# The recurrence's token shift split between ScalarE and VectorE, with a new order table

## The reference, cut to what matters

```
shifted = concatenate([prev[:, None], p[:, :-1]])      # the token before
xs = p + (shifted - p) * mu                            # mu: one weight per projection column
```

## Time and profile before

| what | us |
|---|---|
| median of 3 runs | 2172.32 (2167.52 to 2173.0) |
| the profiled execution's own time | 2170.53 |
| its span, first to last instruction | 2168.6 |
| interleaved stage, layer 1 | 412.8 |
| interleaved stage, layer 2 | 410.8 |

### The profile page before, as it was taken

How to read it: one execution, slowest core, us unless ns; L and a number is a source line. 1 busy time by engine, 2 the same in 40 slices (tenths; PEclk the granted TensorE clock), 3 DMA queues, 4 the chain that set the end, 5 groups by cost and what they waited for, 6 DMA issues and landing times.

```text
span 2168.6 us, 53451 instructions
## 1 busy us (share of the span) xinstructions
PE 1960.5 (90%) x22324; PEld 1804.1 (83%) x22324; DVE 1231.5 (57%) x2034; ACT 702.4 (32%) x1294; POOL 49.2 (2%) x137
## 2 busy tenths in 40 slices
PE   5999999988896999999769998999887979999995
PEld 5999888766696999999769987887666879999995
DVE  3254888887736444452333448888886364444423
ACT  3222333433334232342233223433334332222421
POOL 0000000000000101100000000000000000110000
PEclk9999899998998999999879998999998979999998
DMA  4224733232321323223132256332333212323232
GB/s 181 89 84 144 180 109 105 61 99 83 106 94 45 93 89 97 88 88 98 53 133 89 78 176 160 99 99 71 101 88 110 82 49 89 98 88 96 81 101 79
DMA packets 155835, 214.36 MB, mean 99 GB/s; under 512 B 21569, under 2 KB 121410, under 8 KB 153922
## 3 DMA queue, kind: packets, MB, share of 16 engines
q1 hardware_dynamic: 151682, 208.64, 31.5%
q10 hardware_dynamic: 3904, 2.23, 0.5%
HBM read 202.57 MB, written 16.59 MB: 101 GB/s over the span
## 4 chain that ended last, share of the span: by engine, by line
PE 64%; DVE 18%; SPq 8%; issue 4%; ACT 3%; DMA 3%; DVEq 0%; ACTq 0%; another core or an unknown queue 0%
PE ps L814 17%; PE ps L816 16%; PE ps L815 16%; SPq L704 7%; PE ps L1166 2%; DMA ring<-in_w 1%; DVE arena L1999 1%; PE ps L833 1%; DVE arena L1767 1%; DVE arena L1990 1%; PE ps L834 1%; DVE x L2179 1%; DVE arena L1904 1%; PE ps L1132 1%; PE ps L1047 1%
## 5 line engine op out<-in xcount | busy, mean ns | idle before, releaser
L1678 DVE TENSOR_TENSOR ring_lo<-ring,ring_hi 128x1024 fp32r<-128x1024 f32 x202 | 247.4, 1225 | 679.9 <-ACT ring_hi L1321 679.4
L814 PE MATMUL ps<-hm_hi,ring_hi 128*128 128x260 f32 x1600 | 456.1, 285 | 10.0 <-DVE hm_lo L1685 5.2
L816 PE MATMUL ps<-hm_hi,ring_lo 128*128 128x260 f32 x1600 | 454.7, 284 | 0.0
L815 PE MATMUL ps<-hm_lo,ring_hi 128*128 128x260 f32 x1600 | 453.3, 283 | 0.0
L1321 ACT ACTIVATE ring_hi<-ring 128x1024 fp32r<-128x1024 f32 x202 | 213.8, 1059 | 680.2 <-PE ps L816 615.7
L814 PEld LDWEIGHTS ps<-hm_hi,ring_hi 128*128 128x128 f32 x1600 | 304.1, 190 | 12.5 <-issue 7.3
L816 PEld LDWEIGHTS ps<-hm_hi,ring_lo 128*128 128x128 f32 x1600 | 303.7, 190 | 0.0
L815 PEld LDWEIGHTS ps<-hm_lo,ring_hi 128*128 128x128 f32 x1600 | 303.7, 190 | 0.0
L814 PE MATMUL ps<-in_hi,ring_hi 128*128 128x260 f32 x736 | 211.6, 287 | 6.9 <-DVE ring_lo L1678 6.9
L814 PE MATMUL ps<-hf_hi,ring_hi 128*128 128x260 f32 x704 | 202.1, 287 | 8.8 <-DVE hf_lo L1685 8.2
L816 PE MATMUL ps<-in_hi,ring_lo 128*128 128x260 f32 x736 | 207.8, 282 | 0.0
(11 more groups left out here) (401 smaller groups left out, 3354.5 us busy)
## 6 DMA issues: line engine op xcount, KB each, us to landing
ring<-in_w SPq DMA_DIRECT2D x202, 512.0 KB, 3.5
extra<-in_kv_cmp SPq DMA_DIRECT2D x96, 128.0 KB, 2.3
arena<-in_kv_cmp SPq DMA_DIRECT2D x80, 128.0 KB, 2.4
slot<-in_kv_cmp SPq DMA_DIRECT2D x80, 128.0 KB, 2.9
out_win_old<-in_win SPq DMA_DIRECT2D x16, 511.0 KB, 4.4
arena<-in_k_sel SPq DMA_DIRECT2D x96, 64.0 KB, 1.9
extra<-in_k_sel SPq DMA_DIRECT2D x96, 64.0 KB, 1.9
slot<-in_v_sel SPq DMA_DIRECT2D x96, 64.0 KB, 1.9
```

Source lines behind the costliest of these rows:

```text
L814: mmul(out, wh, hi[:, k, cols], start=(k == 0), stop=False)
L815: mmul(out, wh, lo[:, k, cols], start=False, stop=False)
L816: last = mmul(out, wl, hi[:, k, cols], start=False, stop=(ci == len(chunks) - 1 and k == k1 - 1))
L1678: v.tensor_tensor(ring_lo[:, n % RING, :], r, ring_hi[:, n % RING_HI, :], SUB).then_inc(S["w_lo"], 1)
```

## The change

The token shift becomes `xs = p * (1 - mu) + shifted * mu`. `dif` leaves VectorE. A new ScalarE step `part` computes the first product into the tile `dif`, 14 copies of 128 columns, each scaled by a per-partition operand; `mix` and `mixlow` become 2 and 12 scalar_tensor_tensor of 128 columns, shifted times mu plus `dif`. `mix` waits for `part` on a new semaphore `part1`; `part` of slice sc waits for the key squares of slice sc - 1 (for slice 0: for `rs out`). `1 - mu` is made once per layer by one VectorE instruction into a new tile `rest_mu`; the arena shrinks by 20 columns. The planner's costs: `dif` 4.25 (VectorE) becomes `part` 4.2 (ScalarE), `mix` 0.85 becomes 0.6, `mixlow` 1.9 becomes 2.6.

```
-        put("dif", "DVE", 4.25)
+        put("part", "ACT", 4.2, *([ago("squares")] if sc else []))
-        put("mix", "DVE", 0.85, *([ago("rkv")] if sc else []))
+        put("mix", "DVE", 0.6, *([ago("rkv")] if sc else []), *here("part"))
-        put("mixlow", "DVE", 1.9, *here("mix"))
+        put("mixlow", "DVE", 2.6, *here("mix"))
...
-ORDER = ("008670667870768677066086067707700667767767777666070707668676070667786607700000777701716817177181767106167171718776717171"
+ORDER = ("067680866070870767607678076007676770676767767060867770667768670067676660077006066760870767661671176186610171766767867117"
...
+        rest_mu = sb("rest_mu", [P, RP])
...
-        ARENA = 30900
+        ARENA = 30880
...
-                    if stage == "tanh":
+                    if stage == "part":
+                        if sc:
+                            act.wait_ge(T["x1"], 2 * sc)
+                        else:
+                            act.wait_ge(S["rs_out"], 1)
+                        for i in range(RP):
+                            o.go(A(dif[:, i, :], pr[:, i, sc * SC + 1:(sc + 1) * SC + 1], ACT.Copy, scale=rest_mu[:, i:i + 1]))
+                        o.tell(T["part1"])
+                    elif stage == "tanh":
...
+                o.go(v.tensor_scalar(rest_mu[:], C("mu"), -1.0, 1.0, MUL, ADD))
...
-                    if stage == "dif":
-                        o.do(v.tensor_tensor(dif, pr[:, :, sc * SC:(sc + 1) * SC], pr[:, :, sc * SC + 1:(sc + 1) * SC + 1], SUB))
-                        o.go(v.tensor_tensor(dif, dif, wide(C("mu"), SC), MUL))
...
+                    if stage in ("mix", "mixlow"):
+                        if stage == "mix":
+                            dve.wait_ge(*at_sc("part1", 1))
+                        for i in range(3 * RJ, RP) if stage == "mix" else range(3 * RJ):
+                            o.go(v.scalar_tensor_tensor(xs[:, i, :], pr[:, i, sc * SC:(sc + 1) * SC], C("mu", i), dif[:, i, :], MUL, ADD))
+                        if stage == "mix":
+                            o.tell(T["x1"])
+                        else:
+                            o.settle()
```

More of the change, by code:

```diff
@@ L138, in constants @@
     return c, np.concatenate([cos, sin], 1)
-PER_SC = {"x1": 2, "act1": 2, "lora1": 2, "sig1": 2, "ld_ok": 1, "kk1": 2, "gl_mm": 1, "y_mm": 2, "gg_ok": 1, "rk_ok": 2, "root1": 1, "exp1": 1, "prep": 2,
+PER_SC = {"x1": 2, "part1": 1, "act1": 2, "lora1": 2, "sig1": 2, "ld_ok": 1, "kk1": 2, "gl_mm": 1, "y_mm": 2, "gg_ok": 1, "rk_ok": 2, "root1": 1, "exp1": 1, "prep": 2,
           "gmm": 4, "gmask": 4, "nmm": 1, "inv_q": LEVELS - 1, "inv_qc": LEVELS - 1,
@@ L353, in early_thread @@
     return [(("early", 0, "whi"), "ACT", 1.15, [("smp", 6, "sel_v")]), (("early", 0, "wlo"), "DVE", 1.4, [("early", 0, "whi")])]
-ORDER = ("008670667870768677066086067707700667767767777666070707668676070667786607700000777701716817177181767106167171718776717171"
[L357 to L362, removed]
+ORDER = ("067680866070870767607678076007676770676767767060867770667768670067676660077006066760870767661671176186610171766767867117"
+         "617767617617167776161776276373322672326227233662237672322366722367272662762638216667262712762627118621621617622176826176"
+         "122612166272727762776726278271122721276272672273427277146427672747272786436743232687343767232367762377266683772773716167"
+         "166277767861626671676227776622776662172761276167672627617616827627277616276767268277278676218727226672671622771222687622"
+         "627672466362427241277462764262223682243273328622363782662246662662327832637223611221862116122612712861126218721282622211"
+         "262227277626627626727427272242678727726722276622747767227462662662238276482267363263326722364262726232322487263266272226"
+         "323622262464866744686677645647547776")
 def merged_order():
```

## The result

Over 20 runs each, the changed kernel takes 2175.0 us (2168.7 to 2181.3) and the kernel before 2170.6: ratio 1.0017, 95% interval 1.0009 to 1.0025. It is slower by a little, inside what I called no change and inside the range; the forecast had been faster, 2162.5.

The account below looks back on a forecast made before the run. PE was taken to bound the stage up to win_v 0, SP's load issue most of the rest. Per layer +5.1 - 9.1 = -4.0 us, -8.0 for two, from 2170.5 to 2162.5 us; range 2147 to 2178.

Parts of the forecast that it names:

- The frame: Interleaved stage, once per layer: its end was put 168.2 us behind win_v 0, plus SP's stall ahead of unit 31.
- C: Selected-key softmax, 497.4 to 537.5 us: less VectorE work ahead of sel_v 0 ends SP's stall, -9.1 us a layer (0 to -10.6).
- A: Stage up to win_v 0, at 421.5 us: PE bounds it and gets 8.8 us more, 3.7 taken back: +5.1 a layer.
- VectorE loses 7.2 there and gains 11.5: Ahead of win_v 0: three slices save VectorE 2.4 us each, moved steps add 11.5 by planner's costs; it gets no freer.
- the packing: Stage up to win_v 0: idle PE time (14.9 us) absorbs added steps; a quarter recovered; rival absorbing all 8.8: 2149 us, chance 0.22.
- So I cost it at nothing: VectorE's wait for part at slice 0: about 2.5 us idle, taken as covered by PE's chunks, so 0.
- D: Last five selected loads, 537.5 to 594.5 us: SP issues them as before, so change 0.
- It cancels: Rival: +8.8 us up to win_v 0 against -9.1 to -10.6 from the stall's end; 2167 to 2170 us, chance 0.24.
- The rival of late loads: SP's queue at win_v 0 and unit 31: loads start later, stall stays; 2177.5 to 2188 us, chance 0.12.
- The rival of ScalarE's block on the path: Slices 0 and 1: waiting for ScalarE's copies puts up to 2 x 4.2 us into each layer; 2179 us, chance 0.06.
- the arithmetic of SP: SP's queue from win_v 0: ten loads of 10.7 us each, a 10.6 us stall before unit 31, then five loads.
- the 11.5 us: VectorE work leaving the stretch between sel_k 7 and sel_v 0: 12.1 us by planner's costs, taken as 11.5.

Follow-up runs that it names:

- half of weigh: Changed kernel with the last multiplication of VectorE's weigh step over half of the keys in attention units 0 to 14: 2163.4 us, 0.9982 to the kernel before.
- the doubled block: Changed kernel with ScalarE's 14 copies of slice 0 done twice, 4.2 us more ahead of VectorE's first tail: 2187.1 us, 1.0073 to the kernel before.
- the four kernels that are alike up to unit 21: The changed kernel and three differing from it only behind unit 21; its first load came at 433.53, 431.01, 431.22 and 433.06 us.
- the three of the kernel before: The kernel before and two kernels like it up to unit 21; its first load came at 422.61, 422.34 and 425.19 us.

## Why the prediction was wrong

*The frame held.* The stage's end is counted from SP's loads: unit 21's first load, ten units at 10.6 us, unit 31, then 60 to 63 us. Unit 31 comes at the later of two times, SP's own and sel_v 0. Before, sel_v 0 was the later one; now SP is, by a few microseconds (unit 31 was issued at 539.25, and sel_v 0's matmuls began at 533.74 instead of 537.48).

*C held.* -11.4 and -7.3 against -9.1, and the wait for sel_v 0 is gone. Sel_v 0 does come sooner, as the step said: its products begin 26.3 us behind those of sel_k 7 (507.40 to 533.74) instead of 40.1 (497.42 to 537.48), with VectorE busy 20.9 us in between instead of 31.1. But loads that start 10.9 us later would by themselves have hidden nearly all of the old stall, had sel_v 0 stayed where it was; so its end has two causes here.

*The step that failed is A.* "PE is the tight one", and from it 8.8 us of PE's steps less 3.7 taken back. A measured +10.9 and +10.5, and no idle time of PE came back: 15.2 us (246.0 - 230.78) against 14.9. By PE's busy time alone the sum would nearly close (10.6 us more in the changed kernel); it is the exchange of work that tells the engines apart. Two things were wrong in the step.

First, the tight engine. VectorE is busy 79% of A, and the page's shares made it look free; but its queue moves win_v 0. The chain of the kernel before already ran on it. The pieces of this chain from 187.5 to 422.6 add up to 118 us on VectorE and 80 on PE; between these lines it does not leave VectorE but for the gaps between its instructions:

```profile
329.36 0.69 DVE arena L1762
...
390.50 0.61 DVE nsa L1934
391.21 1.15 PE ps L1036 x32
```

The old operations in the new table (7 us more of VectorE ahead of win_v 0) put it 6.0 us later, half of weigh (6 us less) 4.1 to 7.6 earlier and the end 3.8 a layer, while PE's 8.7 us less brought nothing. The Trainium skill, "Perfetto Trace Analysis", section "Identifying the Most-Contended Engine", says to find the engine with the highest occupancy and to optimize it first, and that for PE the busy share of matmuls is a poor measure of the room left, the share of weight loads a better one. Here PE leads by both, with 94% and 81% of A, the second close to VectorE's 79%, and it is VectorE that moves the event. I had the number in hand, "VectorE loses 7.2 there and gains 11.5", and used it only to weigh the packing. VectorE's busy time ahead of unit 21 rose by 2.5 us (195.06 against 192.60 up to 422.60), although three token shifts had become shorter.

Second, the new wait. "So I cost it at nothing", with 2.5 us if the cover were gone: VectorE waited 2.91 us at slice 0, and the doubled block showed that more of this wait comes out at win_v 0. PE's chunks went on, but the cover had to be VectorE's and there was none. How much would come back without the 2.91 us no run shows.

Together these are 5.4 of the 10.9 us, counted as VectorE's time. The rest, about 5.5, is other idle time of VectorE ahead of win_v 0; it comes with the table behind step 70, and its cause stays open. Where it lies can be said: 4.9 of the 10.9 us are there when rs out ends (in this pair of profiles; in others with the new table it ends up to 2.5 us earlier), and the new table has five attention steps ahead of it (att 2 turn, evac and values, att 3 scores and mask) in place of two chunks of the sample group; 6.0 come behind it, 1.1 of them as work of VectorE, 2.91 as the new wait. PE's clock is not behind these 6.0: between 230 and 270 us it was granted 0.70, 0.79, 0.75 and 0.70 in the four kernels that are alike up to unit 21, and the way from rs out was 189.5 us in each. Ahead of rs out it may have a part (0.83, 0.83 and 0.74 in the three of the kernel before); that was not tested.

*D* was put at 0 and measured +2.4 and +2.1. From the first load of unit 31 to that of unit 35 it is 45.5 us against 44.2; other kernels here with the same five units needed 42.4 to 45.6 in layer 1. I take this part for the scatter of SP's issue; no run tests it. Another 1.0 us in each layer is the new table's: it has the last attention unit's values (L1154) between the last sel_v product and the sample group's last one, which starts 3.77 us behind it instead of 2.79 (timelines of PE, before, then after):

```profile
597.34 1.88 PE L1255 MATMUL ps<-cst,smp 128*128 128x8 f32 x8 [0.85 <-ACTq L421]
...
597.31 1.98 PE L1154 MATMUL ps<-arena 128*64 128x128 f32 x16
599.22 1.88 PE L1256 MATMUL ps<-cst,smp 128*128 128x8 f32 x8
```

*The rivals.* "It cancels" came closest in time (2167 to 2170), but with PE as its reason. The rival of late loads had the first half right: they start later; but the stall went. The rival of ScalarE's block on the path had the right mechanism and the wrong place: slice 0, 2.9 us, and not the whole block twice.

*The prices* of single instructions were right (3.85 and 4.2 us); so was the arithmetic of SP. What they missed is which queue a moved step lengthens. (In the list of what the new order has ahead of win_v 0, mask of att 12 is one too many; it stands there in the old order too, and the 11.5 us are right without it.)

## What to carry to other kernels

When an order table moves a step, price it on every engine that the step uses, and let the engine whose queue holds up the next event decide, not the one with the largest busy share; a run that takes work from one engine alone shows which it is. A new wait of an engine that holds up the next event has to be covered in that engine's own queue; here PE's chunks did not cover it. And where a load queue sets the end, an edit that speeds up the engines can cost time by starting that queue later: shorten the queue first, and the same edit pays (here 4 us, with 12 of 16 pages in the last five units).

## What was not expected of the hardware

Less work for PE went with a lower clock: with 8.7 us of matmuls taken out of A, the granted clock there was 0.89 in layer 1, and PE was still busy for 216.98 of 234 us. The four kernels that are alike up to unit 21 had 0.92 to 0.94 there; in layer 2 it was 0.92 against 0.93, so one profile says little of the size. SP's issue of 16 register-addressed DMAs took between 8.19 and 11.66 us in these runs, 12 of them 6.1 to 9.0, and ScalarE issued four in 1.85 to 3.35 us.
